# A two-layer hybrid decoder trunk: x, vectors and angles of the front in another order, and small moves behind it

## The reference, cut to what matters

```
c_act = silu(c)
for l in range(2):
    mod = c_act @ w_mod[l] + b_mod[l]              # shift, scale and gate of both sub-layers
    sh1, sc1, g1, sh2, sc2, g2 = split(mod, 6)
    h = x * (1 + sc1) + sh1
    q, k, v, qi, ki, wi, xr, yg = split(h @ w_in[l])
    q, k, qi, ki = rope(...)                       # cos and sin of positions * frequency
    attn_out = attention(q, k, v, top-k keys by an indexer from qi, ki, wi)
    xc = causal_conv(xr); lru_out = rg_lru(xc, gates, lambda) * gelu(yg)
    merged = concat(rms_norm(attn_out), rms_norm(lru_out))
    x = layer_norm(alpha * x + (1 + g1) * (merged @ w_out[l]))
    h2 = x * (1 + sc2) + sh2
    x = layer_norm(alpha * x + (1 + g2) * (relu(h2 @ w_up[l]) ** 2 @ w_down[l]))
```

## Time and profile before

| what | value |
|---|---|
| three runs | 1315.83, 1317.0, 1319.31 us; median 1317.0 |
| the profiled execution | 1316.02 us, of which its span is 1314.4 |
| PE busy | 1269.4 us, 97% of the span |
| DVE, ACT, POOL busy | 782.1 (60%), 555.1 (42%), 162.6 us (12%) |
| chain of work that ended last | PE 84%, ACT 5%, DVE 5%, DMA 2% |
| granted PE clock, mean | 0.992 of full speed |

### The profile page before, as it was taken

How to read it: one execution, slowest core, us unless ns; L and a number is a source line. 1 busy time by engine, 2 the same in 40 slices (tenths; PEclk the granted TensorE clock), 3 DMA queues, 4 the chain that set the end, 5 groups by cost and what they waited for, 6 DMA issues and landing times.

```text
span 1314.4 us, 17052 instructions
## 1 busy us (share of the span) xinstructions
PE 1269.4 (97%) x6229; PEld 997.9 (76%) x6229; DVE 782.1 (60%) x1258; ACT 555.1 (42%) x842; POOL 162.6 (12%) x131
## 2 busy tenths in 40 slices
PE   4999999999999999999999999999999999999996
PEld 2766767787888888888887676777778888888885
DVE  2757998756834635537476699876664353434354
ACT  2754557535513313314246535863463242331331
POOL 2000345111000000000120024610100000000012
PEclk9999999999999999999989999999999999999998
DMA  9753445321352343342244444341143323233211
GB/s 314 249 186 122 154 133 169 113 87 41 113 164 92 103 153 96 109 145 96 80 146 157 138 138 145 128 129 49 49 125 99 97 81 110 81 111 96 96 65 65
DMA packets 76471, 158.57 MB, mean 121 GB/s; under 512 B 6529, under 2 KB 14969, under 8 KB 76409
## 3 DMA queue, kind: packets, MB, share of 16 engines
q1 hardware_dynamic: 64064, 112.80, 27.4%
q0 software_dynamic: 11712, 44.57, 10.2%
q10 hardware_dynamic: 632, 0.39, 0.1%
HBM read 155.64 MB, written 2.10 MB: 120 GB/s over the span
## 4 chain that ended last, share of the span: by engine, by line
PE 84%; ACT 5%; DVE 5%; DMA 2%; issue 2%; POOL 1%; POOLq 0%; ACTq 0%; SPq 0%; DVEq 0%
PE bank L659 25%; PE bank L661 24%; PE bank L660 24%; PE bank L624 2%; PE bank L706 2%; DMA first_mod<-in_w_mod_dram 1%; DMA mod_raw<-in_w_mod_dram 1%; PE bank L558 1%; PE bank L856 1%; ACT a_hi L1023 1%; DVE lru_root L1755 1%; POOL w_lo L492 1%; PE bank L890 1%; PE bank L720 1%; ACT resid L1044 1%
## 5 line engine op out<-in xcount | busy, mean ns | idle before, releaser
L1499 DVE TENSOR_TENSOR w_lo<-w_raw,w_hi 128x1024 fp32r<-128x1024 f32 x168 | 206.1, 1233 | 330.3 <-ACT w_hi L1012 330.1
L1012 ACT ACTIVATE w_hi<-w_raw 128x1024 fp32r<-128x1024 f32 x192 | 201.7, 1058 | 449.4 <-PE bank L661 447.2
L659 PE MATMUL bank<-a_hi,w_hi 128*128 128x512 f32 x896 | 361.1, 403 | 3.6 <-DVE a_lo L1541 2.9
L661 PE MATMUL bank<-a_hi,w_lo 128*128 128x512 f32 x896 | 350.6, 391 | 0.0
L660 PE MATMUL bank<-a_lo,w_hi 128*128 128x512 f32 x896 | 350.1, 391 | 0.0
L659 PEld LDWEIGHTS bank<-a_hi,w_hi 128*128 128x128 f32 x896 | 168.7, 188 | 64.2 <-issue 25.3
L659 PE MATMUL bank<-b_hi,w_hi 128*128 128x512 f32 x512 | 200.0, 391 | 0.0
L661 PE MATMUL bank<-b_hi,w_lo 128*128 128x512 f32 x512 | 199.5, 390 | 0.0
L660 PE MATMUL bank<-b_lo,w_hi 128*128 128x512 f32 x512 | 199.5, 390 | 0.0
L661 PEld LDWEIGHTS bank<-a_hi,w_lo 128*128 128x128 f32 x896 | 168.6, 188 | 36.2
L660 PEld LDWEIGHTS bank<-a_lo,w_hi 128*128 128x128 f32 x896 | 169.0, 189 | 34.7 <-issue 1.9
(11 more groups left out here) (256 smaller groups left out, 1410.2 us busy)
## 6 DMA issues: line engine op xcount, KB each, us to landing
mod_raw<-in_w_mod_dram POOLq DMA_DIRECT2D x40, 1024.0 KB, 6.0
w_raw<-in_w_up_dram SPq DMA_DIRECT2D x64, 512.0 KB, 3.7
w_raw<-in_w_down_dram SPq DMA_DIRECT2D x64, 512.0 KB, 3.7
w_raw<-in_w_in_dram SPq DMA_DIRECT2D x48, 512.0 KB, 3.6
first_mod<-in_w_mod_dram SPq DMA_DIRECT2D x8, 1024.0 KB, 13.2
w_raw<-in_w_out_dram SPq DMA_DIRECT2D x16, 512.0 KB, 3.8
x_in<-in_x_dram POOLq DMA_DIRECT2D x4, 512.0 KB, 10.4
out_dram<-y_out SPq DMA_DIRECT2D x8, 256.0 KB, 2.1
```

The costliest lines, as they stand in the source:

```text
L659: mm(o, wh, hi(kk), start=first, stop=False)
L661: last = mm(o, wl, hi(kk), start=False, stop=fin)
L1012: last = af(hi, src, ACT.Copy)
L1499: last = tt(lo, src, hi.bitcast(F32), ALU.subtract)
```

## The change

Nothing that is computed changes but the count of unread matmuls in `layer_norm`. The edits:
1. The four loads of x move from POOL's queue to SP's: in each stage first_mod twice, x, then the qi weights.
2. POOL's loads of the gate blocks (4 of 64 KB) in layer 0 wait for the strips of stage 2 (mod_used 6) instead of standing at the start.
3. ACT issues only c, b_mod, positions and freq ahead of its first sigmoid; the other vectors after it. Its copies of the vectors (vectors_out) come ahead of stage 0's a tiles, not behind stage 0.
4. DVE takes off two of the three parts of 2 pi before stage 1, not all after stage 1; `lambdas` moves from ahead of stage 3 to behind it.
5. POOL's low part lows[10] goes behind the issue of mod_raw piece 13 (it stood ahead of it).
6. `layer_norm`: keep_busy 3 becomes 4, and 2 becomes 3 at the place after the values' sum.
7. PE spreads lrb ahead of turn_tile 0 and 1, and DVE signals its roots ahead of the two root_diag tiles.

```diff
@@ -405,6 +405,8 @@
                 if s == FIRST_STAGES - 1:
                     sp.wait_ge(mod_used, 2)
                 load_first_mod(sp, s, 1)
+                sp.dma_start(xs[:, :, s * 2 * P:(s + 1) * 2 * P], A["x"][0, :, s * 2 * P:(s + 1) * 2 * P]
+                             .rearrange("(n p) d -> p n d", p=P)).then_inc(x_in[s], 16)
                 load_in(0, "qi", s)
 
             def layer(l):
@@ -459,12 +461,6 @@
             gp.affine_select(out=ident[:, :], in_=ident[:, :], compare_op=ALU.not_equal, fill=1.0, base=0,
                              pattern=[[-1, P]], channel_multiplier=1).then_inc(p_const, 1)
 
-            def load_stage(s):
-                pool.dma_start(xs[:, :, s * 2 * P:(s + 1) * 2 * P], A["x"][0, :, s * 2 * P:(s + 1) * 2 * P]
-                               .rearrange("(n p) d -> p n d", p=P)).then_inc(x_in[s], 16)
-
-            for s in range(FIRST_STAGES):
-                load_stage(s)
             gp.memset(causal[:, :], 0.0).then_inc(p_const, 1)
             pool.wait_ge(p_const, 3)
             last_block = causal[:, (TT - 1) * P:]
@@ -477,7 +473,10 @@
 
             def layer(l):
 
-                pool.wait_ge(full_s[7], uses_before(7, "out13", l))
+                if l:
+                    pool.wait_ge(full_s[7], uses_before(7, "out13", l))
+                else:
+                    pool.wait_ge(mod_used, 2 * FIRST_STAGES - 2)
                 for g, name in enumerate(("w_gate_a", "w_gate_x")):
                     for par in range(2):
                         pool.dma_start(blk[64 * par:64 * par + 64, g, :, 64 * par:64 * par + 64],
@@ -498,7 +497,7 @@
                     gp.tensor_tensor(xc[:, m, :], xc[:, m, :], gi[:, m, :], ALU.mult).then_inc(lru_gated, 1)
 
                 lows = [(name, p) for name in POOL_LO for p in range(PAIRS)]
-                lows_after = {7: lows[0:1], 8: lows[1:3], 9: lows[3:5], 10: lows[5:7], 11: lows[7:8], 12: lows[8:11]}
+                lows_after = {7: lows[0:1], 8: lows[1:3], 9: lows[3:5], 10: lows[5:7], 11: lows[7:8], 12: lows[8:10], 13: lows[10:11]}
                 for n in range(LATE_PAIRS):
 
                     pool.wait_ge(mod_used, l * MOD_PAIRS + (NEXT_PAIRS + n + 1 - MR))
@@ -770,10 +769,10 @@
                 pe.wait_ge(ln_q_s, n * (DK - 2) + 2)
                 pe.wait_ge(free_s[4], uses_before(4, "sums" + tail, l))
                 add(TT, ln_q, first=True)
-                keep_busy(3)
+                keep_busy(4)
                 pe.wait_ge(ln_s_s, n)
                 add(0, ln_s)
-                keep_busy(2)
+                keep_busy(3)
                 pe.wait_ge(ln_sq_s, n * DK)
                 add(TT, ln_sq[:, (DK - 1) % 2, :], stop=True).then_inc(full_s[4], 1)
                 pe.wait_ge(free_s[5], uses_before(5, "mb" + tail, l))
@@ -927,10 +926,10 @@
                     return run
 
                 late_mod(l, 14)
+                pe.wait_ge(roots_ready, l * 3 + 1)
+                spread(4, "lrb", l, mix_root[:, 0:TT])
                 turn_tile(0)()
                 turn_tile(1)()
-                pe.wait_ge(roots_ready, l * 3 + 1)
-                spread(4, "lrb", l, mix_root[:, 0:TT])
 
                 late_mod(l, 15)
                 group("out0", l, mix_hi, mix_lo, mix_ready(l * (5 * DK)), order=OUT_ORDER, between={10: turn_tile(2), 12: turn_tile(3)})
@@ -964,17 +963,23 @@
 
 
             act.dma_start(c_rows[:, :], A["c"].rearrange("b (t p) -> (b t) p", p=P)).then_inc(p_in_c, 16)
-            for name, (at, n) in VEC.items():
+            def load_vector(name):
+                at, n = VEC[name]
                 src = A[name]
                 if name == "conv_w":
                     src = src.rearrange("l j (t p) -> (j t) l p", p=P)
                 else:
                     src = src.rearrange("l (t p) -> t l p", p=P)
                 act.dma_start(stage[at:at + n, :, :], src).then_inc(p_in_b if name == "b_mod" else p_in_small, 16)
+
+            load_vector("b_mod")
             act.dma_start(pos[:, :], A["positions"][0:1, :].broadcast_to([P, T])).then_inc(p_in_pos, 16)
             act.dma_start(freq[:, :], A["freq"]).then_inc(p_in_pos, 16)
             act.wait_ge(p_c, 1)
             af(csil[:, :], banks[4][:, 0:DK], ACT.Sigmoid).then_inc(p_sin, 1)
+            for name in VEC:
+                if name != "b_mod":
+                    load_vector(name)
             act.wait_ge(p_b, 1)
             af(vecs[:, 0, 0:6 * DK], banks[1][:, 0:6 * DK], ACT.Copy).then_inc(p_act, 1)
 
@@ -1030,6 +1035,8 @@
                 af(first_rows[:, s % 2, :], banks[7][:, :], ACT.Copy).then_inc(first_rows_s, 1)
                 split_hi("qi", 0, s)
                 act.wait_ge(first_gains, 2 * s + 2)
+                if s == 0:
+                    vectors_out()
                 for kk in (2 * s, 2 * s + 1):
                     src, g, b = banks[5 + kk % 2][:, :], gains[:, 0, kk:kk + 1], gains[:, 1, kk:kk + 1]
                     act.wait_ge(x_turned, kk + 1)
@@ -1069,8 +1076,6 @@
                 if l == 0:
                     for s in range(FIRST_STAGES):
                         first_stage(s)
-                        if s == 0:
-                            vectors_out()
                         if s == 1:
                             lambdas()
                         if s == 2:
@@ -1471,12 +1476,15 @@
                 for n in range(2):
                     step(ts(ang[:, 2 + n, :], ang[:, 2 + n, :], -ROUND, None, ALU.add))
 
-            def angles_reduced():
-
-                for part in TWO_PI:
+            def angles_parts(parts):
+
+                for part in parts:
                     step.settle()
                     for n in range(2):
                         step(stt(ang[:, n, :], ang[:, 2 + n, :], -part, ang[:, n, :], ALU.mult, ALU.add))
+
+            def angles_folded():
+
                 step.settle()
                 for n in range(2):
                     step(ts(ang[:, n, :], ang[:, n, :], PI_IN, -PI_IN, ALU.min, ALU.max))
@@ -1607,11 +1615,13 @@
                     ve.wait_ge(p_act, 1)
                     first_stage(0)
                     angles_turns()
+                    angles_parts(TWO_PI[:2])
                     first_stage(1)
-                    angles_reduced()
+                    angles_parts(TWO_PI[2:])
+                    angles_folded()
                     first_stage(2)
+                    first_stage(3)
                     lambdas()
-                    first_stage(3)
                     ve.sem_inc(mods_out, 1)
                     ve.sem_inc(gains_ready, 1)
                     ve.wait_ge(p_const, 7)
@@ -1880,9 +1890,9 @@
                 mix_vars(1)
                 attn_tile(TT - 1)
                 mix_recips(1, 0, 2 * TT - 1)
+                ve.sem_inc(roots_ready, 1)
                 token_diag(0)
                 token_diag(1)
-                ve.sem_inc(roots_ready, 1)
                 mix_vars(2)
                 lru_merge(0)
                 lru_merge(1)
```

## The result

| kernel | median of its runs, us | before beside it, us | ratio [95% interval] |
|---|---|---|---|
| changed | 1308.13 (1307.17 to 1309.17) | 1317.84 | 0.9917 [0.9900, 0.9934] |
| changed, measured again beside later runs | 1307.62 | 1319.62 | 0.9913 [0.9896, 0.9929] |

The kernel became 9.7 us faster; 1307.0 was forecast. The profiled execution of the changed kernel is one of its longest, 1309.17 us with a span of 1307.5, and that of before one of its shortest, so between the two traces there are only 6.9 us. I account for those, and come back to the difference.

The account below looks back on a forecast made before the run. PE was taken to bound the kernel, with gains only where it idles or runs at lower clock. Front with lambdas -5.8, POOL's queue +1.0, attention's end -3.0, piece 13 -0.8, norms -0.5: -9.1 from 1316.0, so 1307.0 us (1303 to 1310).

Parts of the forecast that it names:

- The loads: Front: first_mod 1's wait of 6.44 us goes, cols of stage 3 at 44.2 against 52.66, a gain of 8.5 us.
- that PE would be late by itself is excluded: Front: PE skips 11.5 us of waits, more than the 8.5 us gain, so PE does not set the pace.
- The lambdas: Ahead of vec_ready: signal 2.7 us later against the stages, PE waits 2.5 us in xr; -5.8 us left with the front.
- rival four: Front: PE held at the lower clock through the whole qi group, slower, 1326 us; chance 0.03.
- POOL's queue: Front: early mod_raw pieces 0 and 1 share bandwidth with x's rest and qi's last pair; +1.0 us, of 0 to 2.8.
- rival one: Front: POOL's bytes flow once issued, x's last quarter and qi's last pair come 5.9 us later; 1311 us; chance 0.13.
- The attention's end: Each layer's attention end: earlier spread removes out0's 1.29 us wait and root_diag's 0.23; -3.0 us, between -3.1 and 0.
- Piece 13: w_mod piece in both layers: earlier issue cuts PE's 1.20 us wait; -0.8 us, between -2.4 and +1; mask could cost 1.4.
- two: Front: vectors land late, strips of stage 1 start 2 to 3 us later; 1309 us; chance 0.08.
- five: Front: no gain, because something else than bytes spaces the loads; the rest alone gives 1311.7 us; chance 0.04.
- three: xr banks not taken in the order read, or piece 13's whole wait goes: -2.5 and -1.6 more, 1303 us; chance 0.10.
- the sign that was set: Front: the prediction is wrong if low clock shows over 20 us there.

Follow-up runs that it names:

- the second experiment: Changed kernel plus unread transposes of the identity on PE in the front's three waits for first_mod, lambdas as changed: 1308.37 us, ratio 0.9920.
- the run with both: Changed kernel with lambdas back ahead of stage 3 and unread PE transposes in the front's waits for first_mod: 1305.01 us, ratio 0.9895.

## Why the prediction was right, and where its steps were off

1. **The loads.** The wait for first_mod 1 shrank from 6.44 to 2.80 us; "that wait goes" was too much. The bytes came near where the sum put them: first_mod 7 at 39.2 (forecast 40.2), x's last quarter at 42.1 (41.7). Both differences have the sign that the gate blocks give, 0.7 us of bytes, which the prediction left ahead of first_mod 7: the first packet of theirs in the trace is at 39.1 us, behind first_mod 7, and they landed from 40.4 to 43.0, beside x's last quarter. But the step "that PE would be late by itself is excluded" failed. It counted all 11.5 us of waits as saved, while 5.8 us of waits stayed, and it took PE's clock from the windows of the earlier trace rows, which give 1.00 for 20 to 30 us. In that trace the first record of the clock is at 30.2 us. The lengths of the strips show what it was: 16 took 1.90 us at 17.56, and in a later row of before, 32 took no more:

```profile
47.30 1.91 PE L582 MATMUL bank<-first_mod,csil_window 128*8 128x256 f32 x32
```

So PE ran at half clock there before, and does again from 19.6 to 26.4 us after the change. The gain at cols of stage 3 is 7.3 and not 8.5 us (7.1 to 8.1 in the five traces with this front); the second experiment shows 44.68 as the bytes' own bound, against 44.2 forecast.

2. **The lambdas.** 2.7 us were forecast, 2.9 came back when they were moved; 0.3 of that is an earlier start of the front in that trace. The chain that was named, vec_ready, w_hi, w_lo, qi_rot, sixteen copies, is the one that binds, and PE's waits of 2.9 us together were forecast as 2.5. At 74.42 the forecast was -4.8 with POOL's part; measured -5.1.

3. **What the sum lacked:** behind those waits the clock fell, for 6.8 us, and PE loses 2.3 of the 5.1 us. The half clock after a wait had been read in the earlier trace rows and priced only as rival four, with another place. Not every execution pays this. Of the eight timed executions of the changed kernel three have a mean granted clock of 0.995 or 0.996; an estimate from that leaves 10 to 13 us at half clock in all, and the last norm alone has 8.4 to 15.2 in the traces, so there is no room for 6.8 us more. They took 1306.9 to 1308.0 us; the two that were profiled, at 0.989, took 1309.2 and 1308.8.

4. **POOL's queue.** +1.0 was taken; here it cost nothing, because PE, late by its clock, reached first_mod 6 only at 41.2 us and POOL issued at 42.56; no packet of piece 0 went before 46.2 us, and qi's last pair had landed at 43.7. The 3.2 us from issue to first bytes are not what the traces have: piece 0 was issued at 48.68 in the kernel before and its first packet went at 50.30, 1.6 us later; in the changed kernel it was 3.6 us. The mechanism is real: in the run with both, PE was 1 to 2 us earlier at stage 3 and POOL 1.9, and ACT waited 1.71 us, for the xr weights and not, as rival one had it, for x and qi's last pair.

5. **The attention's end.** -3.0 forecast. From the probabilities to out0 the difference went from -3.6 to -5.3 in the first layer and from -6.7 to -8.3 in the second, -3.2 together, and the experiment that undid it lost 3.2 to 3.7 in the medians.

6. **Piece 13.** -0.8 forecast, -1.8 measured: each layer won 1.3 us at late_mod(13), of which 0.44 went again at the probabilities, for which PE waits 0.2 us longer than before. The mask that was to meet the low part ran alone, 0.43 us instead of 1.50, so the bound of +1.4 had the wrong sign; with the low part ahead of piece 13 again, it took 1.52 us beside one. The lock of the shared port pair of which the Trainium skill's page "SBUF — State Buffer", section "SBUF: two separate sides", tells fits both lengths; the sum by it, +0.6, fell, because POOL was waiting for PE at that moment.

7. **The norms.** -0.5 forecast, -0.6 measured: +0.5 and +0.5 in the first and third, -1.6 in the second, whose half clock is gone.

8. **Not forecast:** 0.5 us of a new wait for ACT's copies in the second layer's xr group (PE came earlier, ACT did not), and 0.7 to 1.4 us in the front for the new order of ACT's loads, which the sum had at nothing.

9. **Traces and medians.** In the sum the errors cancel only in part: 2.0 us less in the front, 0.5 for the new wait, 1.0 more at piece 13. Up to the third norm the traces differ by 7.8 us where the sum has 9.1, at their ends by 6.9; the medians differ by 9.7. About 1 us of the gap between traces and medians, the step from -7.6 to -6.9 and a little ahead of it, is the last norm: the half clock that every trace shows there begins 10.9 us before the end of before's span, 14.8 before that of the changed kernel's, and anywhere from 8.4 to 15.2 in the other kernels, none of which touches it. The rest is that one execution of each is compared: the profiled one of before lies 1.8 us under its median and that of the changed kernel 1.0 over its own. So it is in part luck that the forecast lies 1.1 us from the median; for its terms the traces are the test.

Of the rivals, one, two and five did not come. For two: PE turned the vectors at 16.60 us without a wait for them. Of three, more gain, piece 13 came, with 1.0 us more than the sum had; the banks of xr were taken in the order that was read. Four, PE at half clock through the whole qi group, did not come either: two stretches of 6.8 us each did. But the sign that was set, low clock over 20 us of the front, was nearly met: by the lengths of the strips PE also ran at half clock from its first matmul at 3.6 us to 16.2 us, where the first record stands, which with 6.8 makes 19 us. In three other traces with this front the first record stands at 24.1 to 26.8 us, and all strips before it have the length of half clock.

## What to carry to other kernels

When loads of a starting stage are brought forward, follow the work that stood in the idle time: sixteen tiny instructions, moved from a place where their engine waited to one ahead of a signal, took back more than half of what the front had won (7.3 us at stage 3, 2.8 behind the xr group), and putting them back was worth 4 to 5 us. Read the clock from the length of equal instructions where the trace has no record of it yet. And when an engine comes earlier, look at which transfers it sets off, and whom these meet.

## What the runs showed of the hardware

- The granted clock fell to 1.2 GHz behind short waits that followed each other, but not each time. Nine of the thirteen kernels other than the one before have two or three waits for a bank in the xr group, 2.4 us apart. In five (the changed kernel in both its traces, the unread work in the front, the low part and the vectors put back) it fell at the end of a wait of 1.45 us or up to 0.6 us behind it, with one of 0.33 to 0.36 us ahead; a third wait, of 0.76 to 1.25 us, came when it had fallen. In two (norms and spread as before) it fell within the third wait, and in the run with both 0.7 us behind waits of 0.96 and 1.45 us. It stayed down for 3.4 or 6.8 us. With x in POOL's queue, waits of 0.36, 1.44 and 1.45 us left it up, and so did one wait of 1.26 us or less, or none, in the four other kernels. So these waits make a fall likely; what decides is not shown.
- Of two queues that both have work, the one with the larger packets moved more. Between 8 and 17 us SP's 581 packets carried 0.71 MB and POOL's 575 carried 2.00; in the run with both, between 44 and 52 us, POOL's packets carry 4 KB and SP's 2, so that POOL again has the larger part, with fewer packets (packets, MB, share of the engines):

```profile
q0 software_dynamic: 456, 1.80, 63.1%
q1 hardware_dynamic: 590, 1.10, 41.0%
```
